# Cached keys laid on 128 partitions as three tiles of (head, width) rows, in a two-layer decoder step

## The chip, the cores and the metric

One core of one Trainium2 chip runs the whole program. The metric is device time in microseconds (us), from the start of the program to its end; less is better. Times of before and of the change are compared as medians of several runs.

## The reference, cut to what matters

The program is one inference step of a two-layer decoder for 256 prompt tokens and 8 single new tokens ("samples"), all in float32. Layer 0 holds sparse attention with 16 query heads of width 96 in 4 key/value groups. For the samples, two of its three parts read cached keys: a window of 512 cached rows, and the 2048 cached rows of the page pool (16 pages of 128 rows for each sample).

```python
def win_attend_cached(qr, qpos, kr, vr, kpos):
    B, Sq = qr.shape[:2]
    qg = qr.reshape(B, Sq, KV_HEADS, HPG, HEAD_DIM)
    s = jnp.einsum('bqghd,bkgd->bqghk', qg, kr) * SCALE
    ...
    p = masked_softmax(s, mask[None, :, None, None, :])
    o = jnp.einsum('bqghk,bkgd->bqghd', p.astype(vr.dtype), vr)
...
def sel_attend(qr, qpos, idx, kb, vb):
    ...
    s = jnp.einsum('bqghd,bgqkld->bqghkl', qg, kg) * SCALE
```

So for each of 8 samples, 4 groups and 4 heads of a group there is a score against each cached key of that group: a product over 96 widths. The rest of the step is large matrix products (input and output projections, squared-ReLU MLPs of width 8192), prompt attention, a causal convolution, pooling and a gating MLP.

## The kernel before, in words

Every engine has one program written out by hand; semaphores order them. The large products run as 89 weight groups: the SP queue loads a 128x2048 piece of weights (`wraw`), ScalarE rounds it (`whi`), VectorE takes the rest (`wlo`), and TensorE multiplies (lines 430 to 432). Groups 0 to 9 are the input projection. Between group 9 and group 10 lies the attention stage, and in it the part that the change touches.

**Units of keys.** The cached keys come in 40 units, u = 0 to 39, each 768 KB: u = 0 to 7 are the window keys of sample u (one transfer on the SP queue, line 309); u = 8 to 39 are four pages of sample u % 8 (two pages on the SP queue, line 314, two on the POOL queue, line 372). They land in `kbuf`, which holds four units. A unit's transfer is issued when the unit four places ahead of it has been used (`k_used`). In `kbuf` the partitions are the 96 widths, and the free axis holds 4 pages x 4 groups x 128 keys.

**Scores of a unit (`keys(u)`, line 594).** Four matmuls, one for each key/value group g. The stationary operand is `qzr[:, r, 32g:32g+32]`, 96 partitions x 32 columns in which only the four columns of sample r are not zero, the moving operand is the group's 512 keys, and the output goes to the 32 partitions 32g to 32g+31 of a `psa` bank. Eight units (eight samples) add up in one bank, so that the 128 partitions of the bank hold (group, sample, head). The trace counts each float32 matmul as two, so a unit is x8 there. VectorE empties the bank after each eight units (line 1683, `k_evac`).

**The queries.** `rows[:, 1, :]` holds the samples' queries, 128 partitions (group, sample, head) x 96 widths. VectorE rotates them (lines 1528 to 1533, `rope_done`), TensorE transposes them to 96 partitions x 128 (line 563, `q_tr`) within weight group 9, and VectorE spreads them into the zeroed `qzr` (line 1571, `qz_done`). The first unit of keys waits for that.

**What stands between the units on TensorE.** TensorE runs its program in order. Between units of keys stand transposes of prompt queries and keys (lines 641, 660), block scores of the prompt (line 672), the compressed part of the samples (line 682), eight products for the prompt's compressed values (line 752, each of which waits for VectorE to have read the last, line 1734), and at the end prompt attention (scores line 766, transposes 775 and 813, outputs 787). VectorE meanwhile works off the 31 taps of the convolution (line 1664), some after each of its other duties. Units of cached values (`vbuf`, line 619) follow the keys in the same manner; they lie on 128 partitions (keys) x 384 and their pages are 128 x 1536 bytes.

Of the kernel before, what the change touches and what calls it, by code (L numbers as in the profile page):

```python
# [19 lines left out]
F32 = mybir.dt.float32  # L20
# [7 lines left out]
NB = 8  # L28
# [6 lines left out]
KW = KVH * HD  # L35
# [33 lines left out]
pg0 pg1 pg2 pg3 ptab_in page_ready page_reduced pg_evac sum_mm sum_copied tok_pair tok_copied ts_ready ts_copied  # L69
gate_tr gate_copied conv_in rows_mm rows_copied rope_done kv_rot q_tr qz_done cmp_mm cmp_p cmp_gs pick_done imp_read lift_done pc_tr pc_copied  # L70
qt_copied ov_mm ov_copied ov_tr ov_turned ocmp_mm ocmp_copied tri_in k0 k1 k2 k3 k_used k_evac win_ready win_exp sel_ready sel_exp
# [11 lines left out]
def build(nc, io):  # L83
    with ExitStack() as ctx:
# [61 lines left out]
        qz = early("qz", [128, NB, 128])  # L146
        qzr = early("qzr", [HD, NB, 128])
        rtmp = early("rtmp", [128, 2, 384])
# [34 lines left out]
        qtmp = nc.alloc_sbuf_tensor_at("qtmp", [128, 2, 384], F32, offset=base + b.at["cprod"] + 3072)  # L183
        kbuf = nc.alloc_sbuf_tensor_at("kbuf", [HD, 4, 4, KVH * 128], F32, offset=base + new.at["wraw"])
        vbuf = nc.alloc_sbuf_tensor_at("vbuf", [128, 5, 4, KW], F32, offset=base + new.at["wraw"])
# [80 lines left out]
        def _(sp):  # L266
# [36 lines left out]
            for u in range(40):  # L303
                if u < 4:
                    sp.wait_ge(s.lo_ready, 4 * (G_EOUT - 1) + u + 1)
                else:
                    sp.wait_ge(s.k_used, u - 3)
                if u < 8:
                    sp.dma_start(kbuf[:, u % 4].rearrange("d q n -> d (q n)"), io.wink[u]).then_inc(kin[u % 4], 16)
                    continue  # L310
                r, c = u % 8, u // 8 - 1
                for q in range(2):
                    i = page_id(r, 4 * c + q)
                    sp.dma_start(kbuf[:, u % 4, q, :], io.selk[bass.ds(i, 1)].rearrange("a d n -> d (a n)")).then_inc(kin[u % 4], 16)

# [28 lines left out]
        def _(pool):  # L344
# [18 lines left out]
            for u in range(8, 40):  # L363
# [5 lines left out]
                for q in (2, 3):  # L369
                    at = PAGES * (u % 8) + 4 * (u // 8 - 1) + q  # L370
                    i = pool.value_load(ptab[0:1, at:at + 1], min_val=0, max_val=io.cmp.shape[0] - 1)
                    pool.dma_start(kbuf[:, u % 4, q, :], io.selk[bass.ds(i, 1)].rearrange("a d n -> d (a n)"))\
                        .then_inc(kin_p[u % 4], 16)
# [38 lines left out]
        def _(pe):  # L412
# [142 lines left out]
            def query_hooks(p, n):  # L555
# [3 lines left out]
                if p == 0:  # L559
                    pe.wait_ge(s.rope_done, 1)  # L560
                    pe.wait_ge(s.qt_copied, 1)
                    mm(psm[0:HD, 0, 0:128], Pm("wckt", parts=HD), qtr[:], start=True, stop=True)
                    nc.tensor.transpose(psm[0:HD, 0, 128:256], rows[:, 1, :], ident).then_inc(s.q_tr, 1)
                if p == 1:
# [15 lines left out]
            def keys(u):  # L580
# [7 lines left out]
                if r == 0:  # L588
                    if c < 2:
                        pe.wait_ge(s.bank_free, 4 * (G_EOUT - 1) + c + 1)  # L590
                    else:
                        pe.wait_ge(s.k_evac, c - 1)
                for g in range(KVH):
                    last = mm(psa[32 * g:32 * g + 32, c % 2, :], qzr[:, r, 32 * g:32 * g + 32],  # L594
                              kbuf[:, u % 4, :, g * 128:(g + 1) * 128], start=(r == 0), stop=(r == NB - 1))
                last.then_inc(s.k_used, 1)
# [849 lines left out]
        def _(dve):  # L1446
# [103 lines left out]
            for n in range(4):  # L1550
# [8 lines left out]
            split(9, 0)  # L1559
            dve.wait_ge(s.rows_copied, 1)  # L1560
            step(V.memset(qzr[:], 0.0))
            dve.wait_ge(s.kv_rot, 2)
            turn = [bc(C(n).rearrange("p (a d) -> p a d", a=1), 128, 3, 48) for n in ("coss", "sins")]
            rope(rows[:, 1:4, 0:48], rows[:, 1:4, 48:96], turn[0], turn[1], rtmp[:, 0, 0:144].rearrange("p (a d) -> p a d", a=3),
                 rtmp[:, 1, 0:144].rearrange("p (a d) -> p a d", a=3)).then_inc(s.rope_done, 1)
            split(9, 1)

# [6 lines left out]
            spread(qz, 0)  # L1574
            spread(qzr, 1)
            split(9, 2)
# [835 lines left out]
```

## Time and profile before

| | |
|---|---|
| median of 3 runs | 2531.58 us (2530.49 to 2543.98) |
| profiled execution, own time | 2528.85 us |
| its span, first to last instruction | 2527.0 us |
| mean granted TensorE clock over the span | 0.967 |
| TensorE matmuls busy | 2430.9 us (96%) |
| VectorE busy | 1567.4 us (62%) |
| ScalarE busy | 1070.9 us (42%) |
| the 40 units of keys, matmuls busy | 66.9 us, from 347.3 to 474 us of the span |

TensorE's matmuls are pipelined and their ends are modelled, so the way to price one is from the start of a group to the start of what follows it. The granted clock is given as a share of 2.4 GHz: 1.00 is the high level, 0.50 the low one (1.2 GHz).

### The profile page before, as it was taken

What the parts mean: (1) busy time and instruction counts of PE and PEld (TensorE: products, weight loads), DVE (VectorE), ACT (ScalarE), POOL (GpSimd) and SP (SyncE); (2) the same over time, 40 slices, a digit from 0 to 9 for tenths busy, and PEclk for the clock granted to TensorE, in tenths of its full rate; (3) what the DMA queues carried; (4) which work ended last, traced back from release to release, by engine and by line L of the source; (5) the groups of instructions that cost most, each with busy time, mean ns of one, the idle gap of its engine ahead of it and who ended that gap; (6) DMA issues with size and microseconds to landing.
All of it is one profiled execution on the core that took longest, in us unless ns stands there. A gap on an engine that the chain in (4) does not pass through costs nothing. (4 is left out here: it accounts for less than half of the span.)

```text
span 2527.0 us, 51230 instructions
## 1 busy us (share of the span) xinstructions
PE 2430.9 (96%) x20546; PEld 2277.6 (90%) x20546; DVE 1567.4 (62%) x2026; ACT 1070.9 (42%) x1271; POOL 92.6 (4%) x180
## 2 busy tenths in 40 slices
PE   5999997888999999999999999999999999999996
PEld 4777881477999999999999999999999999999996
DVE  5777777566677456456455677767754654654656
ACT  2333330344366345345345455445643543533543
POOL 0000003131000000000000010000000000000000
PEclk9999985698999999999999999999999999999998
DMA  8888769797455555555545564444555455545551
GB/s 334 289 307 318 255 178 266 222 292 274 172 204 199 201 183 207 205 197 206 207 175 176 182 220 168 164 166 168 182 183 183 168 181 183 177 176 178 183 181 71
DMA packets 100524, 516.73 MB, mean 204 GB/s; under 512 B 13073, under 2 KB 21329, under 8 KB 53425
## 3 DMA queue, kind: packets, MB, share of 16 engines
q1 hardware_dynamic: 89424, 467.90, 52.3%
q0 software_dynamic: 10976, 47.11, 5.8%
q8 instruction: 87, 1.43, 0.2%
q14 instruction: 37, 0.30, 0.0%
HBM read 508.57 MB, written 18.95 MB: 209 GB/s over the span
## 5 line engine op out<-in xcount | busy, mean ns | idle before, releaser
L1466 DVE TENSOR_TENSOR wlo<-wraw,whi 128x2048 fp32r<-128x2048 f32 x356 | 815.1, 2290 | 613.4 <-ACT whi L1005 613.1
L1005 ACT ACTIVATE whi<-wraw 128x2048 fp32r<-128x2048 f32 x356 | 682.0, 1916 | 1055.7 <-PE psa L432 1049.6
L430 PE MATMUL psa<-xhi,whi 128*128 128x266 f32 (+1 forms) x3632 | 1048.5, 289 | 17.5 <-DVE wlo L1466 15.8
L431 PE MATMUL psa<-xlo,whi 128*128 128x266 f32 (+1 forms) x3632 | 1040.4, 286 | 0.0
L432 PE MATMUL psa<-xhi,wlo 128*128 128x266 f32 (+1 forms) x3632 | 1039.2, 286 | 0.0
L430 PEld LDWEIGHTS psa<-xhi,whi 128*128 128x128 f32 x3632 | 688.9, 190 | 51.5 <-issue 30.3
L431 PEld LDWEIGHTS psa<-xlo,whi 128*128 128x128 f32 x3632 | 689.4, 190 | 0.2
L432 PEld LDWEIGHTS psa<-xhi,wlo 128*128 128x128 f32 x3632 | 686.9, 189 | 0.0
L432 PE MATMUL psa<-hhi,wlo 128*128 128x264 f32 x2048 | 581.4, 284 | 0.0
L431 PE MATMUL psa<-hlo,whi 128*128 128x264 f32 x2048 | 581.3, 284 | 0.0
L430 PE MATMUL psa<-hhi,whi 128*128 128x264 f32 x2048 | 580.9, 284 | 0.0
L430 PEld LDWEIGHTS psa<-hhi,whi 128*128 128x128 f32 x2048 | 385.3, 188 | 0.1
L431 PEld LDWEIGHTS psa<-hlo,whi 128*128 128x128 f32 x2048 | 385.2, 188 | 0.1
L432 PEld LDWEIGHTS psa<-hhi,wlo 128*128 128x128 f32 x2048 | 384.5, 188 | 0.0
L1482 DVE TENSOR_TENSOR page<-page,pe_rep 128x768 f32<-128x768 f32 x128 | 115.9, 952 | 18.9 <-DMA page<-in_cmp 18.5
L1974 DVE COPY gb<-psa 128x2 f32<-128x2 f32 x156 | 23.9, 154 | 113.1 <-PE psa L432 113.1
L594 PE MATMUL psa<-kbuf,qzr 96*32 96x512 f32 x320 | 66.9, 934 | 13.6 <-DMA kbuf<-in_selk 13.6
L1976 DVE SCALAR_TENSOR_TENSOR stage<-mean,gb,psa 128x264 f32<-128x264 f32 x156 | 76.3, 489 | 5.5
L1344 ACT ACTIVATE stage<-stage,gb 128x264 f32<-128x264 f32 x128 | 64.6, 505 | 23.9 <-DVE stage L1978 23.9
L1176 ACT ACTIVATE pp<-pp,hg 128x128 f32<-128x128 f32 (+1 forms) x64 | 28.4, 445 | 108.4 <-DVE hg L1753 108.4
L466 PE MATMUL psm<-page,const 128*32 128x384 f32 x512 | 55.2, 503 | 18.2 <-DVE page L1482 18.2
L1978 DVE TENSOR_TENSOR stage<-stage,rstd 128x264 f32<-128x264 f32 x156 | 67.5, 433 | 5.3
(390 smaller groups left out, 1350.6 us busy)
## 6 DMA issues: line engine op xcount, KB each, us to landing
wraw<-in_w SPq DMA_DIRECT2D x356, 1024.0 KB, 4.8
page<-in_cmp SPq DMA_DIRECT2D x128, 384.0 KB, 4.7
kbuf<-in_selk SPq DMA_DIRECT2D x64, 192.0 KB, 5.2
kbuf<-in_selk POOLq DMA_DIRECT2D x64, 192.0 KB, 5.5
vbuf<-in_selv SPq DMA_DIRECT2D x64, 192.0 KB, 3.9
vbuf<-in_selv POOLq DMA_DIRECT2D x64, 192.0 KB, 4.0
o_win<-in_win POOLq DMA_DIRECT2D x8, 1533.0 KB, 8.6
kbuf<-in_wink SPq DMA_DIRECT2D x8, 768.0 KB, 6.5
```

Of the source, the lines that this page charges most:

```text
L430: mm(out, wh, hi[:, k, 0:w], start=(k == 0), stop=False)
L431: mm(out, wh, lo[:, k, 0:w], start=False, stop=False)
L432: last = mm(out, wl, hi[:, k, 0:w], start=False, stop=(k == KT - 1))
L466: last = mm(psm[c:c + 32, 2, 0:KW], C("blkz", 28 - 4 * r, 60 - 4 * r), page[:, (2 * r + q) % 8, half * KW:half * KW + KW], start=(r == 0), ...
L594: last = mm(psa[32 * g:32 * g + 32, c % 2, :], qzr[:, r, 32 * g:32 * g + 32], kbuf[:, u % 4, :, g * 128:(g + 1) * 128], start=(r == 0), st ...
L1005: A(whi[:, p % 2, :], wraw[:, p, :], ACT.Copy).then_inc(s.hi_ready, 1)
L1176: ins = A(pp[i % 2][:, w * h:w * h + w], pp[i % 2][:, w * h:w * h + w], ACT.Exp, bias=stp[:, c:c + 1], accum_out=stp[:, 16 + c:17 + c])
L1344: A(stage[:, n, :], stage[:, n, :], ACT.Relu, bias=gb[:, n, 1:2]).then_inc(s.relu_done, 1)
L1466: V.tensor_tensor(wlo[:, p % 2, :], wraw[:, p, :], whi[:, p % 2, :].bitcast(F32), ALU.subtract).then_inc(s.lo_ready, 1)
L1482: V.tensor_tensor(v, v, bc(pe_rep[:].rearrange("p a (g d) -> p a g d", g=1), 128, 2, KVH, HD), ALU.mult)\
L1976: V.scalar_tensor_tensor(stage[:, n, :], mean[:], gb[:, n, 0:1], psa[:, n, 0:NT], ALU.mult, ALU.add).then_inc(s.bank_free, 1)
L1978: V.tensor_tensor(stage[:, n, :], stage[:, n, :], rstd[:], ALU.mult).then_inc(s.ev_done, 1)
```

## The change

Cached keys are laid out anew by the host. A page of keys is 4 groups x 96 widths = 384 rows of 128 keys; these rows are cut into three tiles of 128, so that a page is 128 partitions x (3 tiles x 128 keys). Tile 0 holds group 0 and the first 32 widths of group 1, tile 1 the other 64 widths of group 1 and the first 64 of group 2, tile 2 the last 32 widths of group 2 and all of group 3. A page is now 128 x 1536 bytes, before 96 x 2048; the bytes are the same.

A unit's scores are again four matmuls of 512 moving columns, now over 128 partitions: tile 0 against 64 stationary columns (groups 0 and 1, output partitions 0 to 63), tile 2 against 64 (groups 2 and 3, partitions 64 to 127), and tile 1 twice against 32 columns (group 1, partitions 32 to 63, and group 2, partitions 64 to 95), added to what the first two left there.

The queries must follow: VectorE multiplies each query into its own group's 96 of 384 columns (`qsplit`), TensorE transposes that in three pieces of 128 in place of one of 96, and VectorE spreads them with three copies into `qzr` (tiles 0 and 2) and `qzm` (tile 1), which it has zeroed.

```diff
-        qzr = early("qzr", [HD, NB, 128])
+        qzr = early("qzr", [128, NB, 128])
+        qzm = nc.alloc_sbuf_tensor_at("qzm", [128, NB, 64], F32, offset=base + new.at["x"] + NB * KW * 4)
...
-        kbuf = nc.alloc_sbuf_tensor_at("kbuf", [HD, 4, 4, KVH * 128], F32, offset=base + new.at["wraw"])
+        kbuf = nc.alloc_sbuf_tensor_at("kbuf", [128, 4, PIECE], F32, offset=base + new.at["wraw"])
+        qsplit = nc.alloc_sbuf_tensor_at("qsplit", [128, KVH, HD], F32, offset=base + early.at["rtmp"] + 1536)
...
-                    sp.dma_start(kbuf[:, u % 4].rearrange("d q n -> d (q n)"), io.wink[u]).then_inc(kin[u % 4], 16)
+                    sp.dma_start(kbuf[:, u % 4, 0:4 * KW], io.wink[u]).then_inc(kin[u % 4], 16)
...
-                    sp.dma_start(kbuf[:, u % 4, q, :], io.selk[bass.ds(i, 1)].rearrange("a d n -> d (a n)")).then_inc(kin[u % 4], 16)
+                    sp.dma_start(kbuf[:, u % 4, KW * q:KW * q + KW], io.selk[bass.ds(i, 1)].rearrange("a d n -> d (a n)")).then_inc(kin[u % 4], 16)
...
-                    nc.tensor.transpose(psm[0:HD, 0, 128:256], rows[:, 1, :], ident).then_inc(s.q_tr, 1)
+                    pe.wait_ge(s.q_split, 1)
+                    qflat = qsplit[:].rearrange("p g d -> p (g d)")
+                    for t in range(3):
+                        last = nc.tensor.transpose(psm[:, 0, 128 + 128 * t:256 + 128 * t], qflat[:, 128 * t:128 * t + 128], ident)
+                    last.then_inc(s.q_tr, 1)
...
-                for g in range(KVH):
-                    last = mm(psa[32 * g:32 * g + 32, c % 2, :], qzr[:, r, 32 * g:32 * g + 32],
-                              kbuf[:, u % 4, :, g * 128:(g + 1) * 128], start=(r == 0), stop=(r == NB - 1))
+                key = kbuf[:, u % 4, 0:4 * KW].rearrange("p (q t n) -> p q t n", q=4, t=3)
+                for t, lo in ((0, 0), (2, 64)):
+                    mm(psa[lo:lo + 64, c % 2, :], qzr[:, r, lo:lo + 64], key[:, :, t, :], start=(r == 0), stop=False,
+                       skip_group_check=True)
+                for lo in (32, 64):
+                    last = mm(psa[lo:lo + 32, c % 2, :], qzm[:, r, lo - 32:lo], key[:, :, 1, :], start=False, stop=(r == NB - 1),
+                              skip_group_check=True)
...
+            V.memset(qzm[:], 0.0)
             step(V.memset(qzr[:], 0.0))
...
+            dve.wait_ge(s.rope_done, 1)
+            V.tensor_tensor(qsplit[:], bc(rows[:, 1:2, :], 128, KVH, HD),
+                            bc(C("strip").rearrange("p (g a) -> p g a", a=1), 128, KVH, HD), ALU.mult).then_inc(s.q_split, 1)
...
-            spread(qzr, 1)
+            for q, stride, t, lo, off in ((qzr, 132, 0, 0, 0), (qzr, 132, 2, 64, 64), (qzm, 68, 1, 32, 0)):
+                zflat = q[:].rearrange("p a b -> p (a b)")
+                dst = bass.AP(zflat.tensor, zflat.offset + off, [list(zflat.ap[0]), [32, 2], [stride, NB], [1, 4]])
+                ins = V.tensor_copy(dst, psm[:, 0, 128 + 128 * t + lo:192 + 128 * t + lo].rearrange("p (g a b) -> p g a b", g=2, b=4))
+            ins.then_inc(s.qz_done, 1)
```

The pages on the POOL queue change in the same way as those on the SP queue. Nothing else moves.

How the order of TensorE's instructions changes is seen at the units of keys u = 7 to 13 in the attention stage. Before, each unit is four matmuls of 32 output partitions (line 594); lines 682, 689 and 694 are the samples' compressed part.

```order
L672 MATMUL psa<-ckp,qpt 128x8 x8
L594 MATMUL psa<-kbuf,qzr 32x512 x4
L682 MATMUL psm<-psumv,qz 32x96 x32
L594 MATMUL psa<-kbuf,qzr 32x512 x8
L689 MATMUL psm<-const,ovr 96x128
L594 MATMUL psa<-kbuf,qzr 32x512 x8
L694 MATMUL psm<-param,hg 128x96
L594 MATMUL psa<-kbuf,qzr 32x512 x8
L641 MATMUL psm<-const,tok 96x128 x8
```

The same place in the change, up to unit 11 (lines 682, 692 and 699 there are lines 672, 682 and 689 of before):

```order
L682 MATMUL psa<-ckp,qpt 128x8 x8
L601 MATMUL psa<-kbuf,qzr 64x512 x2
L604 MATMUL psa<-kbuf,qzm 32x512 x2
L692 MATMUL psm<-psumv,qz 32x96 x32
L601 MATMUL psa<-kbuf,qzr 64x512 x2
L604 MATMUL psa<-kbuf,qzm 32x512 x2
L601 MATMUL psa<-kbuf,qzr 64x512 x2
L604 MATMUL psa<-kbuf,qzm 32x512 x2
L699 MATMUL psm<-const,ovr 96x128
L601 MATMUL psa<-kbuf,qzr 64x512 x2
L604 MATMUL psa<-kbuf,qzm 32x512 x2
```

A unit that was one set of four matmuls on four separate strips of output partitions is now a set of two on 64 partitions each, and behind it a set of two on 32 that lie inside the first two's partitions; what stands between the units is the same.

VectorE's program where the queries are turned and spread, within weight group 9, before:

```order
L1561 MEMSET qzr 96x1024
L1528 TENSOR_TENSOR rtmp<-rows,const 128x144
L1529 TENSOR_TENSOR rows<-rows,const 128x3x48
L1530 TENSOR_TENSOR rtmp<-rows,const 128x144
L1531 TENSOR_TENSOR rows<-rows,rtmp 128x3x48
L1532 TENSOR_TENSOR rows<-rows,const 128x3x48
L1533 TENSOR_TENSOR rows<-rows,rtmp 128x3x48
L1466 TENSOR_TENSOR wlo<-wraw,whi 128x2048
L1573 MEMSET pcx 128x128
L1571 COPY qz<-psm 96x4x8x4
L1571 COPY qzr<-psm 96x4x8x4
```

And in the change, from the two clearings on (the six rotating instructions between are lines 1538 to 1543):

```order
L1571 MEMSET qzm 128x512
L1572 MEMSET qzr 128x1024
...
L1543 TENSOR_TENSOR rows<-rows,rtmp 128x3x48
L1578 TENSOR_TENSOR qsplit<-rows,const 128x384
L1476 TENSOR_TENSOR wlo<-wraw,whi 128x2048
L1587 MEMSET pcx 128x128
L1585 COPY qz<-psm 96x4x8x4
L1592 COPY qzr<-psm 128x2x8x4 x2
L1592 COPY qzm<-psm 128x2x8x4
```

One clearing and one product come in ahead of a piece of weights (line 1466 before, 1476 in the change), and one copy becomes three.

## Rows read from the trace of the kernel before

**Rows 1.** The page: span, and granted clock in 40 slices (63 us each).

```profile
span 2527.0 us, 51230 instructions
PEclk9999985698999999999999999999999999999998
```

**Rows 2.** Windows: length; busy of PE, PEld, DVE, ACT, POOL; granted clock; DMA; GB/s.

```profile
347.00:381.00 34.00, 33.32 (x295) 21.37 (x293) 30.71 (x69) 6.34 (x18) 5.73 (x11) 0.80 0.76 208
381.00:421.00 40.00, 27.08 (x120) 5.62 (x120) 29.84 (x73) 4.12 (x7) 14.76 (x29) 0.54 1.04 267
421.00:449.00 28.00, 28.00 (x84) 5.59 (x80) 21.27 (x48) 0.00 (x0) 9.23 (x18) 0.50 1.01 264
449.00:475.00 26.00, 26.00 (x127) 11.66 (x124) 15.35 (x33) 6.31 (x22) 5.12 (x10) 0.61 0.84 247
```

**Rows 3.** Waits from 381 to 424 us: who, for whom, us, times, longest.

```profile
PE psa L594 <- DMA kbuf<-in_selk: 13.6, 10, 3.3
```

**Rows 4.** Timeline of TensorE from 347 us (start, us, instruction, count).

```profile
347.26 1.92 PE L594 MATMUL psa<-kbuf,qzr 96*32 96x512 f32 x16
349.12 2.88 PE L701 MATMUL psm<-const,cprod 128*96 128x4 f32 x32
351.93 1.06 PE L594 MATMUL psa<-kbuf,qzr 96*32 96x512 f32 x8
352.93 1.83 PE L641 MATMUL psm<-const,tok 128*96 128x128 f32 x8
...
357.14 1.08 PE L641 MATMUL psm<-const,tok 128*96 128x128 f32 x8
358.06 1.85 PE L672 MATMUL psa<-ckp,qpt 96*128 96x8 f32 x16
```

**Rows 5.** Timeline of TensorE where it waits for keys (in brackets: idle before).

```profile
381.09 1.07 PE L594 MATMUL psa<-kbuf,qzr 96*32 96x512 f32 x8 [0.77 <-DMA kbuf<-in_selk]
...
384.91 1.93 PE L594 MATMUL psa<-kbuf,qzr 96*32 96x512 f32 x8 [2.36 <-DMA kbuf<-in_selk]
...
410.23 1.93 PE L594 MATMUL psa<-kbuf,qzr 96*32 96x512 f32 x8 [3.34 <-DMA kbuf<-in_selk]
```

**Rows 6.** Timeline of TensorE where it doesn't wait.

```profile
418.10 3.64 PE L594 MATMUL psa<-kbuf,qzr 96*32 96x512 f32 x16 [1.51 <-DMA kbuf<-in_selk]
421.67 1.64 PE L752 MATMUL psm<-cvblk,pct 32*128 32x384 f32 x2
423.24 1.94 PE L594 MATMUL psa<-kbuf,qzr 96*32 96x512 f32 x8
425.11 1.64 PE L752 MATMUL psm<-cvblk,pct 32*128 32x384 f32 x2
...
467.32 1.94 PE L594 MATMUL psa<-kbuf,qzr 96*32 96x512 f32 x8
```

**Rows 7.** Windows in which transfers are dense: keys, then values.

```profile
385.00:400.00 15.00, 11.91 (x52) 2.67 (x56) 12.06 (x31) 2.89 (x4) 6.94 (x13) 0.50 1.05 272
540.00:550.00 10.00, 10.00 (x165) 8.28 (x156) 6.52 (x16) 3.03 (x9) 4.45 (x9) 1.00 1.01 335
```

**Rows 8.** DMA issues from 385 to 400 us: count, KB each, median us to landing.

```profile
o_conv_s<-usx POOLq DMA_DIRECT2D x1, 496.0 KB, 9.1
```

**Rows 9.** Timeline of VectorE around the queries, within weight group 9.

```profile
323.17 0.91 DVE L1561 MEMSET qzr<- 96x1024 f32 x1 [0.16 <-issue]
...
329.95 2.29 DVE L1466 TENSOR_TENSOR wlo<-wraw,whi 128x2048 fp32r<-128x2048 f32 x1 [3.81 <-ACT whi L1005]
...
332.69 0.27 DVE L1571 COPY qzr<-psm 96x128 f32<-96x128 f32 x1
334.08 2.29 DVE L1466 TENSOR_TENSOR wlo<-wraw,whi 128x2048 fp32r<-128x2048 f32 x1 [1.12 <-ACT whi L1005]
```

**Rows 10.** Timeline of VectorE between two products of line 752.

```profile
423.42 0.56 DVE L1734 TENSOR_TENSOR otok<-psm,hg 128x384 f32<-128x384 f32 x1
423.90 2.18 DVE L1664 SCALAR_TENSOR_TENSOR stage<-uext,param,stage 128x256 f32<-128x256 f32 x5
```

More of the change, by code:

```diff
@@ L69 @@
 pg0 pg1 pg2 pg3 ptab_in page_ready page_reduced pg_evac sum_mm sum_copied tok_pair tok_copied ts_ready ts_copied
-gate_tr gate_copied conv_in rows_mm rows_copied rope_done kv_rot q_tr qz_done cmp_mm cmp_p cmp_gs pick_done imp_read lift_done pc_tr pc_copied
+gate_tr gate_copied conv_in rows_mm rows_copied rope_done kv_rot q_tr q_split qz_done cmp_mm cmp_p cmp_gs pick_done imp_read lift_done pc_tr pc_copied
 qt_copied ov_mm ov_copied ov_tr ov_turned ocmp_mm ocmp_copied tri_in k0 k1 k2 k3 k_used k_evac win_ready win_exp sel_ready sel_exp
@@ L371, in _ @@
                     i = pool.value_load(ptab[0:1, at:at + 1], min_val=0, max_val=io.cmp.shape[0] - 1)
-                    pool.dma_start(kbuf[:, u % 4, q, :], io.selk[bass.ds(i, 1)].rearrange("a d n -> d (a n)"))\
+                    pool.dma_start(kbuf[:, u % 4, KW * q:KW * q + KW], io.selk[bass.ds(i, 1)].rearrange("a d n -> d (a n)"))\
                         .then_inc(kin_p[u % 4], 16)
@@ L2371 @@
         cmp=v["cache_cmp_kv"][0].reshape(n_pool, 128, KVW),
-        selk=sel[:, :, 0].transpose(0, 3, 2, 1).reshape(n_pool, HD, KVH * 128),
+        selk=sel[:, :, 0].reshape(n_pool, 128, 3, 128).transpose(0, 3, 2, 1).reshape(n_pool, 128, KW),
         selv=sel[:, :, 1].reshape(n_pool, 128, KW),
-        wink=win[:, :, 0].reshape(NB, 4, 128, KVH, HD).transpose(0, 4, 1, 3, 2).reshape(NB, HD, 4 * KVH * 128),
+        wink=win[:, :, 0].reshape(NB, 4, 128, 3, 128).transpose(0, 4, 1, 3, 2).reshape(NB, 128, 4 * KW),
         winv=win[:, :, 1].reshape(NB, 4, 128, KW).transpose(0, 2, 1, 3).reshape(NB, 128, 4 * KW),
```

## The prediction

> **What bounds the kernel now.** I read the page first. TensorE is busy nearly all the span, and its granted clock is high (0.9 and up, the slices' 9s) except in slices 7 to 10, where it falls to 5 to 8 tenths [rows 1]. That dip is the attention stage, from 347 to about 475 us, in which all 40 units of keys lie. So the windows over it come next [rows 2]. From 347 to 381 TensorE has work nearly all the time (33.3 of 34 us) at a mean clock of 0.80. From 381 to 421 it is busy only 27.1 of 40 us. From 421 to 475 it has no idle time at all (28.00 of 28, 26.00 of 26), and the clock is still at the low level, 1.2 GHz, from 421 to 449. The waits say who is late from 381 to 424: the transfers of selected keys, 13.6 us in ten waits [rows 3]. Nothing else holds TensorE in the whole stage, and what comes behind it is in its program order, so the time of this stage is TensorE's work plus those 13.6 us. VectorE is busy 30.7 of 34, 29.8 of 40, 21.3 of 28 and 15.4 of 26 us [rows 2]; it has slack wherever TensorE's share is asked about, except in the first stretch, where it is nearly full and yet doesn't stop TensorE.
>
> **What a unit of keys costs.** Eight instructions in the trace, the two halves of four matmuls on four strips of output partitions. At the high level two units in a row take 349.12 - 347.26 = 1.86 us and one takes 352.93 - 351.93 = 1.00 us [rows 4]. A matmul streams 512 columns twice; if the four stood one behind the other, the unit would take some four times one matmul. At the low level one unit takes 425.11 - 423.24 = 1.87 us and two take 421.67 - 418.10 = 3.57 us [rows 6]: each further set of streams costs 1.70 us, and 0.17 us goes with a change to other work. Of the 40 units 29 run at the low level (u = 3, 4, 7, and the long run from u = 12 at 384.91 to u = 37 at 467.32 [rows 5, 6]), and 11 at the high one. Check: 29 x 1.87 + 11 x 1.00 = 65.2 us, against 66.9 us busy.
>
> **Part 1: the scores (adds).** The four matmuls now overlap in their output partitions: the two on 64 partitions fill all 128, and the two on 32 lie inside them, so that they can only come behind. A unit becomes two sets of streams of 512 columns, where it was one. No row of before has two sets on the same strips except two units in a row, so those price the second set: at the low level between 1.70 us (a set that follows its like) and 1.87 us (a set with a change of shape), at the high level between 0.86 and 1.00 us. Over 29 and 11 units that is 58.8 to 65.2 us. The second set has another strip width than the first, so I take the dearer end but for a little: 63 us. Under nothing is excluded: the streams are as long as before and there are as many of them, on half as many places at once.
>
> The Trainium skill (TensorEngine Tiling (Array Packing), Key Properties) says that tiles of the array run independently of each other, and that a change of tiling mode drains the engine. That the four strips run side by side is what the 1.00 us of a unit shows; whether widths of 64 do so, and what a change between 64 and 32 costs, no row here shows.
>
> **Part 2: the transfers (removes waits).** The bytes stay, 768 KB for a unit. With keys under way and the DMA engines full (share 1.05) 272 GB/s arrive; with values, whose pages already have the new form of 128 x 1536 bytes, 335 GB/s at a share of 1.01 [rows 7]. A unit is 0.786 MB, so 2.89 us before and 2.35 us in the new form. A unit at the low level will hold TensorE 3.4 to 3.74 us: the transfer is then hidden by more than 1 us a unit, and all 13.6 us of waits go. If the clock is high, a unit takes 1.7 to 2.0 us and the transfer still just about hides, with what stands between the units. The Trainium skill (SBUF — State Buffer, Door 1: The DMA port swizzle) says that bandwidth depends on how many SBUF ports the partitions reach, and by its mapping of partitions 96 of them load half of the ports twice as much as the rest. The trace agrees: 272 against 335 GB/s.
>
> **Part 3: the queries (adds, mostly hidden).** VectorE clears 512 columns more (half of the 0.91 us of `qzr`) and makes one product of 384 columns (I take 0.5 us) before the piece of weights at 329.95, ahead of which it sat idle 3.81 us [rows 9]: hidden. Three copies for one add about 0.5 us before the piece at 334.08, ahead of which it sat idle 1.12 us [rows 9]: hidden; if that cover were gone, 0.5 us. On TensorE two transposes more, 0.12 us each by the eight in 0.92 us of line 641 [rows 4]: +0.2 us.
>
> **The sum.** +63 of streams, +0.2 of transposes, -13.6 of waits: +50 us if the clock's levels lie as before. They need not. The long low run begins at 384.91, right behind TensorE's first two waits for keys (0.77 and 2.36 us [rows 5]), and these waits vanish. The next place at which keys are late in any case is u = 20 (3.34 us idle at 410.23 [rows 5]): the POOL queue has 496 KB of convolution state ahead of its half of that unit, 9.1 us to landing [rows 8]. If the high level lasts until there, the eight units u = 12 to 19 cost 1.9 in place of 3.7 us, 14 us less, and the transposes among them 1.5 us less: +34 us. So the likeliest case is +34 to +50, and I take a value nearer to the middle, +40. Against the profiled execution's own 2528.85 us that gives 2569 us. This execution lies 2.7 us (0.1%) under the median of the runs shown, which I leave aside.
>
> Behind 475 us I let the delay go through in full: TensorE's last unit releases VectorE's softmax of the selected scores and the transfers of values, and all of it waits.
>
> **The rivals.**
> *A, no slower: the high level holds through the stage.* For it: the low run set in behind waits for keys, and these go. Then u = 0 to 7 cost about +8 us; u = 8 to 11, 38 and 39 +6; u = 12 to 37 cost 2.0 in place of 1.87, +3; what stands between them gets cheaper (eight times line 752, 1.57 us each [rows 6], to some 0.8; line 641 1.76 to 0.92 [rows 4]; with prompt attention about -13 in all); the waits give -13.6; VectorE and transfers then take back some 3, since VectorE needs 0.56 + 2.18 us between two products of line 752 [rows 10] and a transfer 2.35 us. Sum -6: 2523 us. Against it: from 421 to 449 TensorE doesn't idle at all and stays at 0.50 [rows 2], so that a lack of waits alone did not bring the level back; and in the first stretch, before any wait, the level already dips (a unit's neighbour of line 641 takes 1.76 us at 352.93 and 0.92 us at 357.14 [rows 4]). It decides once the level is high for more than about 25 of the 29 low units. The Trainium skill (TensorE: Matmul & The Clock Gate, HAM oscillation — how this bites in real kernels) ties the fall of the clock to TensorE's gaps while it waits for transfers; by that rule this rival would be the likeliest. The trace agrees at 384.91 and disagrees from 421 to 449. Chance 0.25.
>
> *B, between: high until line 752's products, then low.* Those begin at 421.67 with units at 0.50 now. Units 12 to 23 high save 12 x 1.8 and 2.5 us more against +50: +24 to +28 with a late part; with an early return of the high level at the prompt's transposes, +12. 2541 to 2557, middle 2549. Chance 0.12.
>
> *C, two matmuls on 64 partitions don't run side by side.* Then a unit is three sets or four; each further set costs 29 x 1.7 + 11 x 0.86 = 59 us: 2628 us and more. Nothing in the trace speaks for it but that no 64-wide pair is in it. Chance 0.04.
>
> *D, the change does nothing for the transfers* (they stay at 272 GB/s, 2.89 us): under the low level they are hidden by units of 3.4 us anyway, so it gives the forecast's time; only with A would it cost, about +10. It has no chance of its own.
>
> The likeliest case has the rest, 0.59.
>
> **How the numbers follow.** Likeliest 2569, its own range 2558 to 2584 (with +34 less 5 for an early return to the high level, and +50 with some of line 672's 1.78 us pieces [rows 4] falling into low stretches, +5). The range to hold the time 8 times in 10: from 2520, which takes in A but for its lower edge, to 2586; C and A's edge are left out. A measurement of this kernel can tell about 0.5%, 12.7 us, from no change. Slower by more: the likeliest case, C, and most of B, 0.59 + 0.04 + 0.09 = 0.72. Within: three quarters of A and the rest of B, 0.21. Faster: the part of A in which the second set overlaps its neighbours better, 0.07.
>
> **What would show each step.** In the changed kernel: a unit's first instruction to the next one's at 3.4 to 3.75 us where the clock is 0.50 and 1.7 to 2.0 us where it is 1.00 (part 1; one of 1.9 us at the low level would refute it); TensorE's waits for selected keys under 4 us in all, and over 300 GB/s wherever the DMA share is 1 (part 2); no wait of TensorE for VectorE from 325 to 347 us (part 3); the granted clock from 381 to 475, at 0.5 to 0.65 for the forecast and over 0.9 for A. The prediction is wrong if the clock level follows the waits alone, or if matmuls over 128 partitions that fill the array hold the high level where those over 96 didn't.

## The result and the profile after

The change takes 2521.62 us (median of 7 runs, 2518.2 to 2527.18) where the kernel before, beside it, takes 2534.25 us (7 runs, 2530.49 to 2545.26): a ratio of 0.9943, 95% interval 0.9918 to 0.9967: some 14 us less by the ratio, 12.6 by the medians. Measured once more as an experiment (below) it gave 0.9957 (0.9939 to 0.9974), 11 us less. The forecast was 2569 us, slower. The profiled execution of after has an own time of 2526.37 us and a mean granted clock of 0.982, against 0.967.

The page of after: span, and granted clock in slices of 63 us.

```profile
span 2524.5 us, 51238 instructions
PEclk9999999998999999999999999999999999999998
```

The dip of slices 7 to 10 [rows 1] is gone. The windows of after over the keys, and the one in which transfers are dense (length; busy of PE, PEld, DVE, ACT, POOL; granted clock; DMA; GB/s):

```profile
347.00:381.00 34.00, 34.00 (x223) 18.64 (x225) 27.97 (x64) 5.71 (x16) 3.76 (x7) 0.90 0.53 171
381.00:421.00 40.00, 35.62 (x191) 8.30 (x182) 32.67 (x79) 4.53 (x9) 16.33 (x31) 0.91 0.92 293
421.00:449.00 28.00, 28.00 (x108) 6.87 (x108) 23.17 (x52) 0.00 (x0) 11.26 (x21) 1.00 0.90 288
449.00:475.00 26.00, 25.30 (x156) 10.79 (x152) 16.67 (x40) 8.78 (x32) 4.83 (x9) 1.00 0.89 305
385.00:400.00 15.00, 14.79 (x65) 3.47 (x63) 10.20 (x27) 3.30 (x6) 6.98 (x13) 1.00 0.93 304
```

The clock column is where the result lies: 0.90, 0.91, 1.00, 1.00 where before had 0.80, 0.54, 0.50, 0.61 [rows 2]. The last row says that the transfers bring 304 GB/s, at a DMA share of 0.93, where before they brought 272 at 1.05 [rows 7]. TensorE's waits in after, from 340 to 480 us (us, times, longest):

```profile
PE psa L601 <- DMA kbuf<-in_selk: 4.4, 4, 3.8
```

Against 13.6 us in ten waits [rows 3]. TensorE's timeline in after: the first units, the one long wait, the products between units, and the first weight group behind the stage.

```profile
347.44 1.08 PE L601 MATMUL psa<-kbuf,qzr 128*64 128x512 f32 x4
348.45 1.05 PE L604 MATMUL psa<-kbuf,qzm 128*32 128x512 f32 x4
349.43 1.08 PE L601 MATMUL psa<-kbuf,qzr 128*64 128x512 f32 x4
...
354.56 1.98 PE L601 MATMUL psa<-kbuf,qzr 128*64 128x512 f32 x4
356.46 1.92 PE L604 MATMUL psa<-kbuf,qzm 128*32 128x512 f32 x4
358.31 1.94 PE L651 MATMUL psm<-const,tok 128*96 128x128 f32 x8
...
413.08 1.98 PE L601 MATMUL psa<-kbuf,qzr 128*64 128x512 f32 x4 [3.75 <-DMA kbuf<-in_selk]
414.99 1.92 PE L604 MATMUL psa<-kbuf,qzm 128*32 128x512 f32 x4
416.84 1.97 PE L601 MATMUL psa<-kbuf,qzr 128*64 128x512 f32 x4
418.73 1.05 PE L604 MATMUL psa<-kbuf,qzm 128*32 128x512 f32 x4
...
424.06 0.91 PE L762 MATMUL psm<-cvblk,pct 32*128 32x384 f32 x2
424.90 1.08 PE L601 MATMUL psa<-kbuf,qzr 128*64 128x512 f32 x4
425.91 1.05 PE L604 MATMUL psa<-kbuf,qzm 128*32 128x512 f32 x4
426.89 0.91 PE L762 MATMUL psm<-cvblk,pct 32*128 32x384 f32 x2
...
607.61 0.59 PE L432 MATMUL psa<-xhi,whi 128*128 128x264 f32 x1
```

A unit is two sets, 349.43 - 347.44 = 1.99 us at the high level and 358.31 - 354.56 = 3.75 us at the low one. The wait of 3.75 us at 413.08 is that of u = 20, where the level falls, and by 418.73 it is back. In the whole stretch of keys the level is low for 13.7 us, summed from the trace's record of the clock; before, for 99.0 us. In the profile of the repetition it is low for 3.4 us, and the keys take 119.2 us.

**Where the time went.** The keys, from the first unit's start to the last matmul's, take 122.5 us instead of 126.4. The weight groups begin again at 607.61 instead of 614.55: the stage is 7 us shorter, 3.9 in the keys and 3.2 behind them. The span is only 2.5 us shorter, since the products behind 607 took 4.4 us longer in this execution. That part isn't the change's: in the profile of the repetition it is 2.8 us shorter than before's. So a pair of profiles can't account for 11 to 14 us by medians; what they show alike in both profiles of the change is the stage, 7.1 and 7.6 us shorter.

### The profile page after: what moved, and what is told of

Read it like the earlier page. It is cut to its first block and busy times, and to the rows that moved or that the text cites. A ratio compares the mean times of both kernels' runs of the same rounds, so it can differ in the third digit from the quotient of the medians.

```text
span 2524.5 us, 51238 instructions
## 1 busy us (share of the span) xinstructions
PE 2438.2 (97%) x20548; PEld 2278.1 (90%) x20548; DVE 1568.5 (62%) x2030; ACT 1070.5 (42%) x1271; POOL 94.0 (4%) x180
## 5 line engine op out<-in xcount | busy, mean ns | idle before, releaser
L1896 DVE TENSOR_TENSOR yacc<-psa,yacc 128x264 f32 (+1 forms) x144 | 55.4, 427 | 22.4 <-PE psa L434 22.4
```

The lines of the kernel that those rows point to most:

```text
L1896: V.tensor_tensor(y, psa[:, n:n + 1, 0:NT], y, ALU.add).then_inc(s.bank_free, 1)
```

## The experiments

All were timed against the kernel before on the same chip; times are medians, intervals 95%. They ask three things: what the new transfers are worth alone, what the doubled streams cost alone, and what the clock's level goes by. They come from three chips. The four runs up to the change over 96 rows are from the first, where before took 2532.48 us. Old transfers with zeros, the change widened, and the two kernels in which late stores are the only edit are from the second (2532.18). The change over 96 rows widened, one filled set, the change widened with late stores and the repetition are from the third (2534.09). Where runs of different chips are compared, the ratios are the safer numbers.

### One half of the change each

**New transfers, old scores.** The kernel before with the new layout of the keys, and still one set of four matmuls, over 96 rows of the new tiles; group 3 reads tile 2 as group 2 does, and only group 0 meets its own 96 widths. Against before, at the scores:

```diff
+                key = kbuf[0:HD, u % 4, 0:4 * KW].rearrange("p (q t n) -> p q t n", q=4, t=3)
                 for g in range(KVH):
                     last = mm(psa[32 * g:32 * g + 32, c % 2, :], qzr[:, r, 32 * g:32 * g + 32],
-                              kbuf[:, u % 4, :, g * 128:(g + 1) * 128], start=(r == 0), stop=(r == NB - 1))
+                              key[:, :, min(g, 2), :], start=(r == 0), stop=(r == NB - 1))
...
```

> The keys come in the new form (128 partitions, 128x1536 bytes a page), the scores are the old one set of four matmuls on 32 output partitions over 96 rows (it reads 96 of the 128 rows, so part of the products is left out). A unit takes TensorE 1.0 us at the high clock level and 1.87 us at the low one, and the transfers bring one each 2.35 us. Theory W (the low level is only a consequence of TensorE's waits for keys): the waits come back, 1 us a unit and more at the high level, so the level falls as before near u = 12 and stays low; waits about 5 us in place of 13.6, whole time 6 to 9 us under before. Theory L (the level follows how much of the time TensorE streams, waits or not): the same fall, the same time. Rival R (the faster transfers are all that the change is worth): the time is that of the change, 12 us under before.

Measured 2524.93 us, ratio 0.9962 (0.9938 to 0.9985). Its waits, then its windows:

```profile
PE psa L595 <- DMA kbuf<-in_selk: 12.6, 9, 3.1
```

```profile
400.00:421.00 21.00, 18.16 (x64) 3.47 (x64) 17.76 (x42) 0.38 (x1) 8.58 (x16) 0.50 0.96 323
421.00:449.00 28.00, 28.00 (x98) 8.07 (x98) 20.50 (x46) 3.09 (x13) 8.58 (x16) 0.50 0.77 234
```

The transfers are faster (323 GB/s), but a unit of one set still takes TensorE less time than its transfer, so that it waits 12.6 us, where about 5 were expected. The gain of about 10 us comes with a long low stretch that sets in later (398.6 against 383.8 us) and ends sooner (456.7 against 469.1): with the shorter ones, 75 us at the low level against 99. From 421 to 449 TensorE idles not at all, and the level stays at 0.50.

**Old transfers, new scores.** The change's two sets over 96 of the old layout's rows; the operands are not the reference's.

```diff
-        kbuf = nc.alloc_sbuf_tensor_at("kbuf", [128, 4, PIECE], F32, offset=base + new.at["wraw"])
+        kbuf = nc.alloc_sbuf_tensor_at("kbuf", [HD, 4, PIECE], F32, offset=base + new.at["wraw"])
...
-                    mm(psa[lo:lo + 64, c % 2, :], qzr[:, r, lo:lo + 64], key[:, :, t, :], start=(r == 0), stop=False,
+                    mm(psa[lo:lo + 64, c % 2, :], qzr[0:HD, r, lo:lo + 64], key[:, :, t, :], start=(r == 0), stop=False,
...
```

> The change's two sets of matmuls for a unit (64, 64, then 32, 32 output partitions), but over 96 rows and from keys that come in the old form, 96 partitions x 2048 bytes a page (which widths meet which queries is not the reference's). A unit takes TensorE 2.0 us at the high level; the transfers bring one each 2.89 us, so 0.7 to 0.9 us of waits a unit between u = 12 and u = 24, over 8 us in all. Theory W (waits alone bring the level down): low from about u = 12 on, units at 3.75 us, time 35 to 50 us over before. Theory L (the level follows how much of the time TensorE streams): about 70% of the time streams, the level stays high for most of the stage, time within 8 us of before and 5 to 10 us over the change.

Measured 2568.21 us (2566.86 to 2573.82), ratio 1.0126 (1.0095 to 1.0156): almost the forecast's number, and with the forecast's picture of a level that holds until u = 20 and is then lost. Its windows:

```profile
385.00:410.00 25.00, 20.73 (x91) 4.83 (x87) 17.94 (x45) 3.90 (x7) 11.10 (x21) 1.00 0.98 254
423.00:447.00 24.00, 24.00 (x50) 4.21 (x48) 7.81 (x17) 0.38 (x1) 5.60 (x11) 0.50 0.65 188
447.00:505.00 58.00, 58.00 (x128) 14.25 (x126) 24.36 (x54) 6.44 (x22) 10.33 (x21) 0.50 0.51 154
```

From 385 to 410 TensorE waits for nearly every unit and keeps the high level; the level falls at 413 and then stays low until 505, over 80 us of it a stretch in which TensorE has work without a gap. Theory W has the time about right, but not its way: it had the level low from u = 12 on.

**The old form twice.** Before's four matmuls, each issued a second time (the sums are twice the reference's).

```diff
+                for again in range(2):
+                    for g in range(KVH):
+                        last = mm(psa[32 * g:32 * g + 32, c % 2, :], qzr[:, r, 32 * g:32 * g + 32],
...
```

> Before, with each unit's four matmuls issued twice (the scores come out doubled). Transfers in the old form, strips of 32, 96 rows: only the amount of streaming is that of the change. Theory W: waits for keys as in before, low from about u = 12, units at 3.6 us, 35 to 50 us over before. Theory L: high for most of the stage, within 8 us of before. If this one and the run with the change's shapes and old transfers differ by more than 5 us, the strip width itself matters.

Measured 2531.66 us, ratio 0.9982 (0.9960 to 1.0004): twice the streams, and no time. In its profile the level is low for 30.7 us of the keys; in that of before, whose operands and transfers are the same, for 99.0. So here the doubled streams alone bring most of the level back. Its windows, then rows of its timeline:

```profile
385.00:410.00 25.00, 19.39 (x167) 5.82 (x159) 19.92 (x51) 3.89 (x7) 11.07 (x21) 1.00 1.03 274
413.00:423.00 10.00, 8.51 (x42) 1.50 (x36) 6.26 (x16) 0.00 (x0) 2.05 (x4) 0.50 1.02 270
423.00:447.00 24.00, 22.56 (x160) 6.30 (x156) 18.59 (x42) 0.38 (x1) 9.53 (x19) 1.00 1.03 272
```

```profile
399.88 1.92 PE L595 MATMUL psa<-kbuf,qzr 96*32 96x512 f32 x16 [1.47 <-DMA kbuf<-in_selk]
402.76 1.92 PE L595 MATMUL psa<-kbuf,qzr 96*32 96x512 f32 x16 [0.95 <-DMA kbuf<-in_selk]
```

A wait of about 1 us ahead of each unit, a unit of 1.9 us, and the level is high. It falls near u = 20 as in the run above, but here it is back by 424 (and is low once more from 447 to 461). Between the two runs neither transfers nor the number of sets differ. What differs is the widths: two sets of four strips of 32 columns, all 128 columns of the array each time, against two strips of 64 and then two of 32, of which the second covers 64 columns and has another width than the first.

### What of the array the streams cover

**The change over 96 rows.** The change with its matmuls over the first 96 partitions; a quarter of each sum is left out.

```diff
-                key = kbuf[:, u % 4, 0:4 * KW].rearrange("p (q t n) -> p q t n", q=4, t=3)
+                key = kbuf[0:HD, u % 4, 0:4 * KW].rearrange("p (q t n) -> p q t n", q=4, t=3)
...
-                    mm(psa[lo:lo + 64, c % 2, :], qzr[:, r, lo:lo + 64], key[:, :, t, :], start=(r == 0), stop=False,
+                    mm(psa[lo:lo + 64, c % 2, :], qzr[0:HD, r, lo:lo + 64], key[:, :, t, :], start=(r == 0), stop=False,
...
```

> The change with the matmuls over 96 of its 128 rows (32 rows of each tile are left out of the products); transfers and order as in the change. Theory A (a filled array, 128 rows, holds the high level): the level falls again, 30 us and more over the change. Theories W and L: as the change, within 3 us, granted clock from 421 to 449 us at 1.00.

Its six runs fall in two groups, 2521.86 and 2525.99 us, and 2560.13 to 2576.02 us; no ratio can be given. Each run's own mean granted clock goes with its group: 0.985 and 0.982, against 0.962 to 0.968. At 0.982 of a span of 2524 us the clock costs 45 us against the high level throughout, at 0.967 of 2558 us 84 us, so that by this estimate the difference between the groups is time at the low level. Where in the kernel it lies no trace shows, for only the lower group has a profile, and in that the level is lost elsewhere: it is low from 371 to 388 us, where TensorE had no wait, comes back, and doesn't fall near u = 20, behind waits of 1.31 and 2.05 us.

```profile
413.00:423.00 10.00, 6.22 (x28) 1.13 (x26) 9.76 (x23) 0.00 (x0) 3.95 (x8) 1.00 1.04 326
```

So four of six runs go as Theory A has it and two as the change does. What decides between them stays open, and the change itself, whose seven runs lie within 9 us, wasn't timed beside them.

**Old transfers, second set filled with zeros.** The run of 2568 us with its second set widened from 32 to 64 columns on each half. The added columns are zero, and the streams as long as before.

```diff
-        qzm = nc.alloc_sbuf_tensor_at("qzm", [128, NB, 64], F32, offset=base + new.at["x"] + NB * KW * 4)
+        qzm = nc.alloc_sbuf_tensor_at("qzm", [128, NB, 128], F32, offset=base + new.at["x"] + NB * KW * 4)
...
-                for lo in (32, 64):
-                    last = mm(psa[lo:lo + 32, c % 2, :], qzm[0:HD, r, lo - 32:lo], key[:, :, 1, :], start=False, stop=(r == NB - 1),
+                for lo in (0, 64):
+                    last = mm(psa[lo:lo + 64, c % 2, :], qzm[0:HD, r, lo:lo + 64], key[:, :, 1, :], start=False, stop=(r == NB - 1),
...
```

> The run with the change's two sets over 96 rows and old transfers, with one edit: the second set is two matmuls on 64 output partitions each, as the first, the added columns of the stationary operand being zeros (they add 0 to two strips). Streams, durations (2.0 us a unit at the high level) and transfers stay. Theory F (what brings the level back after a gap is how much of the array the streams cover; the second set on 64 of 128 columns covers half): the level recovers after the gap near u = 20, as in the run with the old form issued twice; time within 8 us of before, that is 25 to 40 us under the run with the narrow second set. Theory N (changes between strip widths, or the amount of streaming alone): 2568 us again, or for the change of widths some 5 us less at the same low level.

Measured 2531.13 us (2525.15 to 2538.48), ratio 0.9995 (0.9978 to 1.0012): 37 us by the medians, 33 by the ratios, under the same kernel without the zeros, which ran on another chip. Its windows:

```profile
417.00:430.00 13.00, 12.88 (x32) 3.37 (x30) 2.72 (x7) 0.38 (x1) 2.56 (x5) 0.50 1.03 257
430.00:447.00 17.00, 17.00 (x64) 4.66 (x60) 15.57 (x36) 0.00 (x0) 6.15 (x12) 0.99 0.98 266
```

The level falls at u = 20 (without the zeros, within u = 19) and is back by 430. The products that count, the transfers and the length of every stream are alike in this pair. One rival to the reading by columns is left in it: the zeros also take away the change of width within each unit and behind it. That change of width alone doesn't keep the level down, since the change has it too and gets the level back at 418.73; but no run keeps the width and fills the columns otherwise.

**The change over 96 rows, widened.** The same edit on the run of two groups.

> The run of the change over 96 rows, whose times fell in two groups (2522 to 2526 and 2560 to 2576 us), with the second set widened by zeros to 64 and 64 output partitions. Theory F: the level comes back behind every gap, one group of times only, all within 2512 to 2532 us. If rows matter as much as columns: two groups again, or the slow one alone.

Measured 2520.23 us (2512.22 to 2521.65, one group), ratio 0.9938 (0.9913 to 0.9962). None of the six is in the upper group; they ran on another chip than the run of two groups.

**The change, widened.** The same edit on the change itself.

> The change with the second set widened by zeros to 64 and 64 output partitions; the output is the reference's. Theory F: the level was high in the change already but for 6.8 us behind the gap at u = 20 and 6.8 us at the start; now at most 3 us of it are saved: 0 to 4 us under the change. Rival: columns of zeros cost something (longer weight loads, 64 in place of 32 columns): 40 x 2 x 0.03 = 2 us over the change.

Measured 2518.32 us, ratio 0.9942 (0.9920 to 0.9963), the change's within the intervals. Its timeline:

```profile
417.29 0.91 PE L762 MATMUL psm<-cvblk,pct 32*128 32x384 f32 x2
418.13 1.08 PE L601 MATMUL psa<-kbuf,qzr 128*64 128x512 f32 x4
419.04 1.03 PE L604 MATMUL psa<-kbuf,qzm 128*64 128x512 f32 x4
420.00 0.91 PE L762 MATMUL psm<-cvblk,pct 32*128 32x384 f32 x2
```

From product to product 2.71 us, where after takes 426.89 - 424.06 = 2.83: a unit whose two sets have the same width is 0.12 us shorter. That is near 5 us over 40 units, which the time doesn't show.

**One filled set.** The change without its second set; a third of the products is left out.

```diff
-                for lo in (32, 64):
-                    last = mm(psa[lo:lo + 32, c % 2, :], qzm[:, r, lo - 32:lo], key[:, :, 1, :], start=False, stop=(r == NB - 1),
-                              skip_group_check=True)
...
```

> The change without its second set (tile 1, a third of the products, is left out): new transfers, one set of two matmuls on 64 output partitions over all 128 rows. A unit takes 1.0 us at the high level against 2.35 us for its transfer, so TensorE waits more than 1 us a unit. Theory F with waits (the level falls at a gap and comes back if the streams that follow cover the array, waits or not): with half the time idle it stays low for much of the stage from u = 12 on; at the low level a unit takes 1.87 us and little is lost, so the time is 7 to 12 us under before. If the level stays high all the same: over 12 us under before.

Measured 2516.78 us, ratio 0.9922 (0.9896 to 0.9949). Its windows:

```profile
381.00:421.00 40.00, 29.70 (x82) 7.88 (x82) 38.40 (x91) 3.86 (x6) 17.56 (x34) 0.71 0.98 324
421.00:449.00 28.00, 28.00 (x78) 9.38 (x76) 21.61 (x47) 4.02 (x16) 9.53 (x18) 0.62 0.80 244
```

Neither expectation has both halves of this: the level sinks (0.71 and 0.62, and 50 us low in the keys), and the time is still some 20 us under before by the ratio. With a third less to do TensorE waits 14.4 us, and the whole second set, 40 times about 1 us at the high level, costs only the 5 to 9 us between this run and the change's two (0.9943 and 0.9957, with intervals that meet this one's).

### The stores ahead of u = 20

**The change with the stores late.** The two convolution stores go behind the last unit of keys on the POOL queue.

```diff
-                if u == 20:
-                    pool.wait_ge(s.glu_done, 8)
-                    pool.dma_start(io.o_conv_p, uext[:, :, SEQ:SEQ + CONV_W - 1]).then_inc(s.stored, 16)
-                    pool.dma_start(io.o_conv_s, usx[:].rearrange("p c b w -> p (c b w)")).then_inc(s.stored, 16)
...
```

> The change with the two stores of convolution state (60 and 496 KB) moved on the POOL queue from ahead of unit 20's pages to behind the last unit of keys. If the 3.75 us gap at u = 20 and the 6.8 us of low level behind it come from these stores: the gap goes (under 1 us), no low stretch near 412 us, time 4 to 8 us under the change. If keys would be late there anyway: no change.

Measured 2523.02 us, ratio 0.9968 (0.9948 to 0.9987). Its waits, then a window:

```profile
PE psa L600 <- DMA kbuf<-in_selk: 1.7, 3, 0.8
```

```profile
381.00:421.00 40.00, 37.88 (x157) 8.37 (x157) 34.35 (x83) 4.28 (x8) 17.88 (x34) 1.00 0.96 320
```

So the stores are the cause of the long wait: with them late the longest wait is 0.8 us. The fall near 412 goes with it, and the level is low for only 3.4 us in the keys. Yet the time isn't lower than the change's, where 4 to 8 us were expected. One place that takes some back is the end of the stage: there TensorE waits 3.2 us for VectorE's `stage` (line 857), in after 0.5 us.

**Before with the stores late.** The same edit on the kernel before.

> Before with the same two stores moved behind the last unit of keys. The gap of 3.34 us at u = 20 and some of the next two (1.88, 1.51 us) go: waits for keys 9 to 10 us in place of 13.6. The level is low from u = 12 on without them, so it stays: 3 to 5 us under before. If the stores' gap is what keeps the level low from there on, it would come back and the time fall by 15 us and more.

Measured 2533.26 us, ratio 1.0005 (0.9983 to 1.0027). The waits are 9.6 us and the level is as low as ever (99.0 us); the 3 to 5 us expected didn't come.

**The change widened, with the stores late.**

> The change with the second set widened and the convolution stores moved behind the last unit of keys; the output is the reference's. The gap at u = 20 goes and the keys end some 5 us earlier than with the wide set alone, but the stage behind did not pass such gains on when either edit was made alone: 2514 to 2519 us, the same as with the wide set alone within 2 us. If the gains add up: 2510 us or less.

Measured 2515.17 us (2508.73 to 2517.98), ratio 0.9921 (0.9897 to 0.9945), the lowest of the versions that compute everything. Its windows over the keys and over the values behind them:

```profile
421.00:449.00 28.00, 28.00 (x121) 9.87 (x118) 24.53 (x54) 5.00 (x20) 12.00 (x23) 1.00 0.91 291
474.00:590.00 116.00, 100.80 (x1624) 80.72 (x1623) 67.06 (x168) 52.63 (x158) 34.52 (x64) 0.89 0.84 279
```

The level is never low in the keys (0.0 us), though TensorE waits nine times for them, 5.0 us in all and 1.5 at most. Part of that is given back behind them: the keys take 112.7 us, 9.8 less than in after, the whole stage only 5.1 less, and the clock over the values is 0.89.

**The change again,** on the third chip.

> The change itself, unchanged, beside the others on the same chip: 2521 us, 10 to 15 us under before; widened second set alone 2 to 4 us under it.

Measured 2523.38 us, ratio 0.9957 (0.9939 to 0.9974). The widened version with late stores is 8 us under it, with intervals that overlap.

## Why the prediction was wrong, point by point

**What bounds the stage** was read rightly: TensorE's work, the clock under it, and the waits for keys.

**Part 1, the prices.** Right: a unit is two sets, 1.99 us at the high level (forecast 1.7 to 2.0) and 3.75 at the low one (3.4 to 3.75). The pair on 64 partitions runs side by side (1.01 us for the pair, 349.43 - 348.45 = 0.98 for the pair on 32), so rival C is out.

**Part 1, the number of units at each price.** This is where it failed, with the step "+50 us if the clock's levels lie as before" and its likeliest case of +34 to +50. Of 40 units only some two and a half run low, not 21 to 29. By the prices above that is 37.5 x 1.99 + 2.5 x 3.75 = 84 us, against 65 before: +19 where +63 stood. What stands in the step's place: the streams themselves move the level. Before's own four matmuls issued twice, with nothing else changed, cut the low time in the keys from 99.0 to 30.7 us, and the change cuts it to 13.7. The change's two sets need the rest of the change for it: over 96 rows on old transfers they are low for 99.0 us again, and there the forecast's time comes true. The forecast took the level of before as given and let only the waits move it.

**Part 2.** Right in the mechanism: 304 GB/s instead of 272, and waits of 4.4 us, only that of u = 20 a long one, as forecast ("under 4 us" was 0.4 too low). Its worth is larger than the waits. With the wide second set over 96 rows, which keeps the products alike, old transfers give 0.9995 and new ones 0.9938: 14 us, of which 4.5 are waits (9.0 against 4.5). Where the rest lies wasn't found. Nor did a run separate the number of partitions from the length of a piece (2048 against 1536 bytes), which change together.

**Part 3.** Right, by VectorE's timeline in after:

```profile
323.21 0.48 DVE L1571 MEMSET qzm<- 128x512 f32 x1
...
326.87 0.56 DVE L1578 TENSOR_TENSOR qsplit<-rows,const 128x384 f32<-128x384 f32 x1
330.09 2.29 DVE L1476 TENSOR_TENSOR wlo<-wraw,whi 128x2048 fp32r<-128x2048 f32 x1 [2.66 <-ACT whi L1015]
...
334.23 2.29 DVE L1476 TENSOR_TENSOR wlo<-wraw,whi 128x2048 fp32r<-128x2048 f32 x1 [0.71 <-ACT whi L1015]
```

Of the idle 3.81 and 1.12 us [rows 9], 2.66 and 0.71 are left, and TensorE waits for nothing from 325 to 347 us. The first unit starts at 347.44 instead of 347.26, but in the profile of the repetition at 346.64, so that the +0.2 of the transposes is below what two profiles can tell.

**Behind 475 us.** That a delay goes through in full was right: with old transfers and new scores the keys take 165.4 us, 39 more than before, and the whole stage 306.1, 39 more.

**Rival A** is what happened, in its mechanism. Its +17 for the streams came out at +19, and its -13.6 of waits at -9.2. What is left of the keys' 3.9 us, 122.5 - 126.4 - 19 + 9.2 = -14 us, stands against its -13 for the work between the units and its +3 taken back, -10 together. That its 2523 us lies next to the 2521.62 measured is in part luck. It is 6 us under 2528.85, the profiled execution's own time, but the median of before in this comparison is 2534.25, and the change is 12.6 us under that.

**Why A was given only 0.25.** Two arguments were set against it. One, that from 421 to 449 a lack of waits didn't bring the level back, was a true observation of a kernel whose streams were of another kind: one set a unit, and between the units products over 32 rows, for nearly half of the time (1.57 of 3.44 us [rows 6]). The forecast carried its level over to a kernel in which the streams are twice as many. The other, that the level dips in the first stretch before any wait, holds for the change as well: it is low there for 6.8 us (354.56 and 356.46 above), with TensorE busy 34.00 of 34 us. But in the repetition it isn't (clock 1.00 from 347 to 381), and it said nothing of the 26 units from u = 12 to 37. Three theories can now be told apart.

- *The level follows the waits alone.* Fallen. With waits of about 1 us ahead of each unit it stays high (old form twice, and both runs of two sets on old transfers, 385 to 410 us), and without a gap it stays low for over 80 us (narrow second set) and for 28 us (old scores).
- *It follows how long TensorE streams, whatever the streams cover.* Fallen as the only cause. The narrow and the zero-filled second set stream equally long, and differ by 37 us (33 by the ratios).
- *It goes also by how much of the array the streams cover.* The runs are in line with it, and don't prove it. On old transfers, 96 rows with 128 and then 64 columns don't get the level back behind u = 20, and 96 rows with 128 and 128 do, as strips of 32 or of 64. On new transfers 96 rows with a narrow second set gave two groups of times; 128 rows with it (the change) and 96 with the wide one gave one. If it is so, columns of zeros count, since the pair of 2568 and 2531 us differs by nothing else but the change of width. One set alone, over 96 rows (before) or 128, loses the level.

The Trainium skill (TensorE: Matmul & The Clock Gate, HAM oscillation — how this bites in real kernels) ties the fall to gaps while TensorE waits for transfers. The trace of after agrees at 413.08 (the level falls within the wait of 3.75 us), and with the stores late both are gone; it doesn't agree at 353.8, where the level falls and TensorE had no gap. The return is the part that the runs add: it didn't come with the end of the gaps, and it came with more streams (the old form twice).

**What stays open.** Whether the level goes by the columns covered or by the changes of width isn't settled, nor what splits the runs over 96 rows. The values' part gives back some of what the keys gain: it is low for 31.9 us in after, 35.3 in the repetition and 36.2 before, and for 38.7 to 42.3 in the change widened, with late stores, and with both, whose keys end first. In each of these profiles TensorE waits for ScalarE's `ptp` right behind the keys, 5.5 us before and 5.9 in the others, and the level falls in that wait. Nothing was tried against it. Nor is it settled where the 4 to 7 us lie between the stage's gain in the profiles and the gain of the medians, nor why the change with late stores, whose keys take 116.4 us, isn't faster; its interval overlaps the change's.

## What to carry to other kernels

Where TensorE runs a stretch at the low level, its busy time there is no price: more streams on the same work may cost nothing, as long as they bring the level back, so forecast the level first and multiply afterwards. Where transfers make TensorE wait, try matmuls widened with zero columns, and try it alone. It brought 33 to 37 us where the level was lost, and nothing measurable in the change, where it was held already. A level read off the old kernel holds only for its streams; where a change alters rows, columns or the number of sets, give both levels a case with a near equal chance.

## What the runs showed of the hardware

- The same matmuls issued twice took no time (2531.66 against 2532.48 us), because the level was low for 30.7 us of the keys instead of 99.0.
- Zero columns in the stationary operand were worth 37 us (2568.21 against 2531.13; 33 by the ratios) at equal stream lengths.
- The lack of gaps alone didn't bring a low level back: 0.50 from 447 to 505 us with TensorE busy 58.00 of 58, and 0.50 from 421 to 449 with 28.00 of 28 (one set, new transfers).
- Two matmuls on 64 output partitions run side by side: four instructions of 512 columns in 1.01 us at the high level, 1.90 at the low one (348.45 - 347.44, 356.46 - 354.56). A second set of another width costs 0.12 us more than one of the same (2.83 against 2.71 us).
- On 128 partitions of 1536 bytes for each page the DMA engines bring 300 to 333 GB/s between 385 and 400 us wherever they are dense, on 96 partitions of 2048 bytes 245 to 273.
- One kernel can have two times on the same chip, 40 us apart (2521.86 to 2525.99, and 2560.13 to 2576.02); the mean granted clock of the runs, 0.982 and 0.985 against 0.962 to 0.968, accounts for the difference.
